# Eight forgetting-attention heads taken in pairs on TensorE, and one norm moved ahead of a weight split

## The reference

```
q, k, v, f_logit, cx, cb, cc, px, gate_logit = split(rmsnorm(x) @ w_in)
c = cumsum(log_sigmoid(f_logit + forget_b))            # 8 heads of 64
for the query blocks [0,128) (keys [0,128)) and [128,256) (keys [0,256)):
    p = softmax(q k^T / 8 + c_q - c_k, causal);  a = p @ v
y_attn = a @ w_attn_out
y_conv = (cb * conv3(cc * cx)) @ w_conv_out
y_pool = pooled_differences(px)[4 groups of 64] @ pool_w[group] * scale
g = sigmoid(gate_logit)                                # 3 x 1024
x = x + (g0*y_attn + g1*y_conv + g2*y_pool) @ w_o;  then a gated FFN
```

## Time and profile before

| | us |
|---|---|
| median of three runs | 1649.47 |
| the profiled execution, its own time | 1651.84 |
| its span, first to last instruction | 1650.0 |
| PE busy | 1585.8 |
| DVE busy | 1117.6 |
| ACT busy | 812.5 |
| POOL busy | 113.9 |

### The profile page before, as it was taken

How to read it: one execution, slowest core, us unless ns; L and a number is a source line. 1 busy time by engine, 2 the same in 40 slices (tenths; PEclk the granted TensorE clock), 3 DMA queues, 4 the chain that set the end, 5 groups by cost and what they waited for, 6 DMA issues and landing times.

```text
span 1650.0 us, 28888 instructions
## 1 busy us (share of the span) xinstructions
PE 1585.8 (96%) x12134; PEld 1485.1 (90%) x12134; DVE 1117.6 (68%) x1412; ACT 812.5 (49%) x1064; POOL 113.9 (7%) x107
## 2 busy tenths in 40 slices
PE   7999989999999999999988999999999999899998
PEld 6999989999899998999887989998999999789997
DVE  5767667775666767877577476666777756665554
ACT  5545444444545444444468454444455555454442
POOL 1040000000103000000011000000111102000000
PEclk9999999999999999999999899999999999899999
DMA  8765456667675636665632257675887655335652
GB/s 287 251 216 188 164 198 213 200 231 242 217 256 192 200 133 238 213 235 194 227 121 82 98 164 248 228 253 179 272 277 249 208 170 178 104 107 200 195 176 90
DMA packets 230497, 325.56 MB, mean 197 GB/s; under 512 B 7416, under 2 KB 195296, under 8 KB 230368
## 3 DMA queue, kind: packets, MB, share of 16 engines
q1 hardware_dynamic: 223304, 313.00, 56.3%
q10 hardware_dynamic: 7064, 10.71, 2.0%
HBM read 314.23 MB, written 9.45 MB: 196 GB/s over the span
## 4 chain that ended last, share of the span: by engine, by line
PE 77%; DVE 9%; ACT 5%; issue 4%; DMA 4%; POOL 1%; SPq 1%; DVEq 0%; ACTq 0%; POOLq 0%
PE bank L516 24%; PE bank L517 23%; PE bank L518 23%; DVE wlo L1576 2%; ACT whi L1117 2%; DMA raw<-in_w_in 1%; DMA raw<-in_w_ffn_in 1%; PE bank L559 1%; PE bank L593 1%; PE bank L925 1%; PE bank L909 1%; POOL rstd L1049 1%; PE bank L725 1%; PE bank L940 1%; DMA lbias<-forget_sums 1%
## 5 line engine op out<-in xcount | busy, mean ns | idle before, releaser
L1576 DVE TENSOR_TENSOR wlo<-raw,whi 128x2048 fp32r<-128x2048 f32 (+1 forms) x241 | 550.7, 2288 | 261.1 <-ACT whi L1117 260.9
L1117 ACT ACTIVATE whi<-raw 128x2048 fp32r<-128x2048 f32 (+1 forms) x241 | 456.0, 1895 | 119.1 <-PE bank L518 84.9
L516 PE MATMUL bank<-hT_hi,whi 128*128 128x256 f32 x1728 | 494.1, 286 | 6.9 <-DVE hT_lo L1691 3.0
L517 PE MATMUL bank<-hT_lo,whi 128*128 128x256 f32 x1728 | 488.8, 283 | 0.0
L518 PE MATMUL bank<-hT_hi,wlo 128*128 128x256 f32 x1728 | 488.8, 283 | 0.0
L516 PEld LDWEIGHTS bank<-hT_hi,whi 128*128 128x128 f32 x1728 | 331.1, 192 | 14.1 <-issue 10.1
L517 PEld LDWEIGHTS bank<-hT_lo,whi 128*128 128x128 f32 x1728 | 331.4, 192 | 1.2
L518 PEld LDWEIGHTS bank<-hT_hi,wlo 128*128 128x128 f32 x1728 | 331.3, 192 | 0.0
L516 PE MATMUL bank<-whi,hT_hi 128*128 128x256 f32 (+1 forms) x944 | 273.2, 289 | 5.3 <-DVE wlo L1576 2.5
L517 PE MATMUL bank<-wlo,hT_hi 128*128 128x256 f32 (+1 forms) x944 | 268.5, 284 | 0.0
L518 PE MATMUL bank<-whi,hT_lo 128*128 128x256 f32 (+1 forms) x944 | 268.3, 284 | 0.0
(11 more groups left out here) (280 smaller groups left out, 1525.5 us busy)
## 6 DMA issues: line engine op xcount, KB each, us to landing
raw<-in_mlp_w SPq DMA_DIRECT2D x64, 1024.0 KB, 5.7
ada_raw<-in_ada_w SPq DMA_DIRECT2D x96, 512.0 KB, 6.7
raw<-in_w_in SPq DMA_DIRECT2D x44, 1024.0 KB, 5.6
raw<-in_w_ffn_in SPq DMA_DIRECT2D x44, 1024.0 KB, 5.2
raw<-in_dil_w_in SPq DMA_DIRECT2D x36, 1024.0 KB, 5.5
raw<-in_w_ffn_out SPq DMA_DIRECT2D x22, 1024.0 KB, 4.8
raw<-in_w_o SPq DMA_DIRECT2D x8, 1024.0 KB, 5.2
biasb<-head_bias ACTq DMA_DIRECT2D x16, 512.0 KB, 4.6
```

The source lines that it names most:

```text
L516: pe.matmul(dst, lh, rh, start=start, stop=False)
L517: pe.matmul(dst, lh, rl, start=False, stop=False)
L1117: act.activation(view(whi[c % SPL], c), view(raw[c % RAW], c), ACT.Copy).then_inc(s_hi, 1)
L1576: dve.tensor_tensor(view(wlo[c % SPL], c), view(raw[c % RAW], c), view(whi[c % SPL], c).bitcast(F32), ALU.subtract).then_inc(s_lo, 1)
```

## The change

Heads and pooled groups are taken in pairs, the two of a pair in turn on two halves of the array: scores and pooled products on the two halves of its rows, values on the two halves of its columns. The values product swaps its operands, so its result comes out transposed, and `turn_pair` falls away; for this the probabilities are scaled by the inverted sums before they are transposed, with a semaphore `s_pn1` on which PE now waits. The four attention gates come last, with nothing between them. On ACT, `scores` splits the next chunk's weights before the exponentials. In `dilated`, `norm_probs` of the last pair stands ahead of `values(LAST, 0)` and `project_out(2, 3, 4, 5)`.

```diff
-            for i in range(H1 + 3):
-                if i < H1:
-                    begin_head(i)
-                if i <= H1:
-                    fill()
-                if 1 <= i <= H1:
-                    turn_probs(i - 1)
-                if i % 4 == 0:
-                    fill()
-                for gi in {3: (0,), 4: (1,), 5: (2, 3)}.get(i, ()):
-                    pool_branch(gi)
-                if 2 <= i < H1 + 2:
-                    values(i - 2)
-                if i in (4, 6, 8):
-                    turn_pair((i - 4) // 2)
-            last_gate(left.pop())
+            scores(0, left[0])
+            fill()
+            for p in range(H1 // 2):
+                norm_probs(p)
+                fill()
+                if p == 3:
+                    pool_branches(1)
+                turn_probs(p)
+                if p < H1 // 2 - 1:
+                    scores(p + 1, left[0])
+                if p == 2:
+                    pool_branches(0)
+                fill()
+                values(p)
+            while left:
+                fill()
...
             scores(LAST, 1, None)
             project_out(0, 1)
+            norm_probs(LAST, 1)
             values(LAST, 0)
             project_out(2, 3, 4, 5)
-            norm_probs(LAST, 1)
             turn_probs(LAST, 1)
```

On PE:

```diff
+                def scores(p, _):
+                    bks = [begin("a", ("S", unit1(l, 2 * p + h))) for h in range(2)]
+                    for q0, q1, c0 in ((0, P, 0), (P, S, P)):
+                        for h in range(2):
+                            rows = slice(64 * h, 64 * h + 64)
+                            m = pe.matmul(bks[h][:, c0:c0 + q1], qT1[rows, p, q0:q1], kT1[rows, p, 0:q1], start=True, stop=True)
...
+                def turn_probs(p):
+                    for h in range(2):
+                        u = unit1(l, 2 * p + h)
+                        pe.wait_ge(s_pn1, u + 1)
+                        bk = begin("a", ("T", u))
+                        for k in range(3):
+                            m = pe.transpose(bk[:, P * k:P * k + P], P1[h][:, P * k:P * k + P], ident[:, :])
...
+                def pool_branches(gp):
...
+                    bks = [begin("a", ("YP", l, 2 * gp + r)) for r in range(2)]
                     for half in range(2):
+                        for r in range(2):
+                            rows = slice(64 * r, 64 * r + 64)
+                            m = pe.matmul(bks[r][:, S * half:S * half + S], poolw[rows, gp, P * half:P * half + P],
+                                          pd[rows, gp, :], start=True, stop=True)
...
+                def values(p):
+                    for h in range(2):
+                        emptied(pe, ("T", unit1(l, 2 * p + h)))
+                    pair = unit1(l, 2 * p) // 2
+                    bk = begin("a", ("OT", pair))
+                    for t, kts in enumerate(((0,), (0, 1))):
+                        for kt in kts:
+                            for h in range(2):
+                                m = pe.matmul(bk[64 * h:64 * h + 64, P * t:P * t + P],
+                                              V1[:, kt, HD * (2 * p + h):HD * (2 * p + h) + HD],
+                                              PT1[h][:, P * (t + kt):P * (t + kt) + P], start=kt == 0, stop=kt == kts[-1])
```

On ACT and DVE:

```diff
+                def scores(p, following):
+                    split_ahead(("CO", l) if following is None else ("G", l, following))
+                    for h in range(2):
...
+                        exps(u, lambda t: L1[h][:, segs[t][0]:segs[t][1]], lambda t: P1[h][:, segs[t][0]:segs[t][1]])
...
+                def norm_probs(p):
+                    for h in range(2):
+                        u = unit1(l, 2 * p + h)
+                        dve.wait_ge(s_exp, 2 * u + 2)
+                        if u >= 2:
+                            dve.wait_ge(s_pn1, u - 1)
+                        dve.reciprocal(rz[:, h, :], zsum[:, h, :]).then_inc(s_rz, 1)
+                        dve.wait_ge(s_rz, u + 1)
+                        for t, (a, b) in enumerate(segs):
+                            ins = dve.tensor_scalar(P1[h][:, a:b], P1[h][:, a:b], rz[:, h, t:t + 1], None, ALU.mult)
+                        ins.then_inc(s_pn1, 1)
```

More of the change, by code:

```diff
@@ new lines, in values @@
+                def values(p):
[9 more added lines that the diff above has]
+                                              PT1[h][:, P * (t + kt):P * (t + kt) + P], start=kt == 0, stop=kt == kts[-1])
+                    end(m, ("OT", pair))
@@ L694, in _ @@
                 emptied(pe, ("qkT", 4 * l + 1))
-                forgetting_heads(begin_head, gate, conv_out, turn_probs, pool_branch, values,
-                                 lambda p: turn_pair(unit1(l, 2 * p) // 2),
-                                 lambda c: gate(c, lambda: turn_pair(unit1(l, 6) // 2)))
+                forgetting_heads(scores, gate, conv_out, idle, turn_probs, pool_branches, values)
                 for h in range(0, H1, 2):
@@ L1273, in _, with gate @@
                 act.activation(aT_hi[:, 4:6, :], cvb[:, :, :], ACT.Copy).then_inc(s_cvhi, 1)
-                def gate(c, between=idle):
+                def gate(c):
                     split_ahead(("G", l, c))
-                    between()
                     bk = full(act, ("G", l, c))
@@ L1295, in pool_branch @@
[L1295 to L1303, removed]
@@ L1308, in _ @@
+                forgetting_heads(scores, gate, lambda: split_ahead(("CO", l)), idle, turn_probs, pool_branches,
+                                 lambda p: at_high(unit1(l, 2 * p) // 2, p))
                 for c in range(2):
@@ L1824, in _, with scores @@
                 segs = ((0, P), (P, 3 * P))
[L1826 to L1839, removed]
+                def scores(p, _):
+                    for h in range(2):
+                        u = unit1(l, 2 * p + h)
+                        bk = full(dve, ("S", u))
+                        dve.wait_ge(s_lbias, u + 1)
+                        if p:
+                            dve.wait_ge(s_exp, 2 * (u - 2) + 2)
+                        for t, (a, b) in enumerate(segs):
+                            ins = dve.tensor_tensor_reduce(L1[h][:, a:b], bk[:, a:b], lbias[:, 2 * p + h, a:b], 1.0, NEG,
+                                                           ALU.add, ALU.max, mx[:, h, t:t + 1])
+                            if t == 0:
+                                link(ins)
+                        ins.then_inc(drain_sem(("S", u)), 1)
+                        emptied(dve, ("S", u))
+                        dve.tensor_scalar(nmax[:, h, :], mx[:, h, :], -1.0, None, ALU.mult).then_inc(s_nmax, 1)
@@ L1859, in conv_out, with pool_branches @@
                     split_ahead(("CO", l))
[L1861 to L1874, removed]
+                def pool_branches(gp):
+                    for gi in (2 * gp, 2 * gp + 1):
+                        emptied(dve, ("YP", l, gi))
+                        emptied(dve, ("G", l, 8 + gi))
+                        m2 = mg[:, 2 * gi:2 * gi + 2, :]
+                        dve.scalar_tensor_tensor(out=m2, in0=m2, scalar=1.0, in1=mt[gi % 2][:, :, :], op0=ALU.add,
+                                                 op1=ALU.mult).then_inc(s_ypused, 1)
+                forgetting_heads(scores, lambda c: split_ahead(("G", l, c)), conv_out, norm_probs, idle, pool_branches,
+                                 lambda p: at_low(unit1(l, 2 * p) // 2, p))
                 for c in range(1, 4):
```

90 lines of the change are left out of this document (37 added, 53 removed).

## The result

| | before | after |
|---|---|---|
| median of the timed runs, us | 1649.12 (1648.12 to 1651.09) | 1632.12 (1629.21 to 1633.72) |
| profiled execution, us | 1651.84 | 1629.21 |
| its span, us | 1650.0 | 1627.4 |

The ratio is 0.9894, 95% interval 0.9876 to 0.9911: 17.0 us faster, 2.7 more than the 14.3 forecast, and inside the range. The two profiled executions are 22.6 us apart. That is more than the medians, since the one of before is 2.7 above its median and the one of after 2.9 under its own.

A forecast was written before the change was run, and what follows sets the result against it. PE, busy 96% of the span, was taken as the bound. The terms 17.0 + 1.5 - 8.2 - 0.8 + 4.8 gave 14.3 us less, 1635.2 us for the median (chance 62%), range 1629 to 1642.

The forecast's parts named there:

- PE work, 17.0: Both forgetting layers: paired scores, values, pooled products and fewer tile changes save PE 8.5 us a layer, 17.0 in both.
- Old waits, 1.5: Second forgetting layer: PE's waits of 0.85 (low part of G10) and 0.69 us (weights' ring bank) both go.
- The new wait, 8.2: PE waits for DVE's scaling before pair 0's transposes: 3.2 us in the first layer, 5.0 in the second.
- none at pairs 2 and 3: Forgetting layers: PE does not wait for scaling there, as DVE finishes about 3 us before PE wants it.
- the 11 us: Upper size of the new wait over both layers, if each pair 0 scaling waits out a POOL sum.
- Clock in the second layer, 0.8: PE's clock may fall during the second forgetting layer's new wait: 0 to 3 us lost, 0.8 taken.
- The last pair, 4.8: Block 4's last dilated pair: PE's wait falls from 7.85 to 3.7 us; saving 4.2 to 6.2, 4.8 taken.
- the lower bound, 4.2: Block 4's last pair: low end of the 4.2 to 6.2 us saving, used where the clock stays low.
- (a): Small new wait of 5.4 us, clock held in both places: 19.3 us saved, 1630.2 us; chance 15%.
- (b): Long new wait of 11 us, low clock in second layer and block 4: 8.7 saved, 1640.8 us; chance 15%.
- (c): Array halves do not run together for these shapes: 14.3 us of saving gone, 1649.5 us; chance 4%.
- (d): The wait on `s_pn1` repeats at every pair, at 3.5 us a pair 28 lost: slower, 1655 us; chance 4%.

The follow-up runs named there:

- POOL held: Changed kernel with POOL held after each forgetting layer's first two biases until DVE has scaled the first pair: 1627.33 us, ratio 0.9857.
- the last pair alone: Kernel before with only the move of the last dilated pair's normalization: 1644.51 us, ratio 0.9976.
- the run with the low part first: Changed kernel, last dilated pair scaled ahead of chunks 0 and 1, DVE's low part and ACT's copies ahead of their splits: 1624.57 us, ratio 0.9846.
- the two parts timed alone: Changed kernel with the last dilated pair's normalization put back, 1633.44 us (15.5 faster); kernel before with only that move, 1644.51 us (4.5 faster).
- the run with the first pair scaled early: Changed kernel with DVE scaling each forgetting layer's first pair ahead of G10's low part and ada row: 1630.70 us.

## Why the prediction was right, and where it was off

- **PE work, 17.0 us.** Right. The stretches of the forgetting layers are 15.4 us shorter in the traces. The old waits of 1.5 are in this, and the small ones of 0.34 and 0.19 a layer, 1.1 in all, which the prediction left out. Against it stands the new wait, 3.3 as listed. The list misses a part of it: pair 0's transposes hold PE for 1.13 and 1.31 us up to the next group, where pairs 1 and 2 take 0.75, and so does pair 0 with POOL held. That is 0.4 and 0.6 more for head 1's scaling, of which 0.3 is listed. Counted so, the new wait is 3.9 and the work 15.4 - 1.5 - 1.1 + 3.9 = 16.7. The group times came out as worked out: scores of a pair 0.86 (0.85), values 0.81 (0.82), pooled pair 1.06. What the prediction did not see is that the values need their turns.
- **Old waits, 1.5.** Both gone. But they belong to late biases as much as to the code: in the other trace of the old order (the last pair alone) they stand in the first layer, 0.63 and 0.69, where the biases came 6.3 us behind PE's first scores, and not in the second, where it was 4.0. Where the biases come sooner, this term is worth nothing.
- **The new wait, 8.2.** This is the mis-sized term: 3.3 here, and 2.9 to 3.6 in the seven more traces of kernels that leave this wait as it is. The place, the cause and "none at pairs 2 and 3" were right. Of the 4.9 too many, 3.1 are in the second layer and 1.8 in the first.
  - Second layer, head 0: 3.7 forecast, 1.6 measured. The biases came 1.9 us behind PE's first scores (475.44 against 473.52), not 6.5, and DVE came to them from its convolution work: head 0's maximum stood 1.4 sooner than the earlier trace rows gave. The low part took 2.28, not 2.74, which is 0.5. PE came to the wait 0.15 later. The ada row (2.11) and the scaling of head 0 with its reciprocal (1.36 for 1.4) were sized rightly.
  - Head 1, both layers: 1.3 forecast each; 0.3 listed in the second and none in the first, 0.6 and 0.4 by the distances above. Its scaling took 0.73 and 0.55, and PE spends 0.55 on head 0's transposes meanwhile.
  - First layer, head 0: 1.9 forecast, 1.4 measured.

  The 6.5 was one execution. The old code has 4.0 in its other trace, and the twelve traces with the changed forgetting code have 1.3 to 2.6 in nine and 4.1 to 6.2 in three. Whether the change itself brings the biases forward, or only chance does, stays open.
- **POOL beside DVE.** The row (0.71 against 0.17) was read rightly as slowing, and holding POOL shows it: 0.55 against 1.35 for the same scaling. One scaling did wait for a pooled sum. In after's second layer, DVE's and POOL's timelines:

```profile
486.54 0.91 DVE L1852 TENSOR_SCALAR P<-P,rz 128x128 f32<-128x128 f32 x1
487.37 0.34 DVE L1852 TENSOR_SCALAR P<-P,rz 128x256 f32<-128x256 f32 x1
...
485.41 1.95 POOL L1082 TENSOR_TENSOR s<-s 128x540 f32<-128x540 f32 x1
```

The first instruction takes 0.91 where it takes 0.29 with POOL held, and the next begins at 487.37, when POOL's sum ends (485.41 + 1.95 = 487.36). DVE met the last 0.8 us of the sum, not the whole. No scaling of pair 0 in these traces was over 1.42 us, though POOL's sums are up to 3.0 long, so the 2.2 a head behind the 11 us did not come. The Trainium skill ("SBUF — State Buffer", "SBUF: two separate sides") has the two engines lock each other out for a whole instruction. At this place the trace agrees; what the forecast had too long is how much of POOL's instruction is left when DVE comes.
- **Clock in the second layer, 0.8.** Did not come: the granted clock is 1.00 from 484 to 492 us, through the wait of 1.6. The clock term was small either way.
- **The last pair, 4.8.** 3.8 in the traces and 4.5 timed. The wait fell to 3.7 as worked out; the clock fell in it, and the transposes stayed at 3.81. The earlier trace rows had said so: eight transposes in 1.94 after 3.71 idle are 0.24 each, the pace of sixteen in 3.81, where the full clock gives sixteen in 1.91 (the run with the low part first). The windows of the kernel before show the lower level there:

```profile
905.00:906.00 1.00, 0.00 (x0) 0.00 (x0) 0.97 (x5) 0.00 (x0) 0.00 (x0) 0.63 0.00 0
...
908.00:909.00 1.00, 1.00 (x6) 0.96 (x5) 0.64 (x3) 0.00 (x0) 0.00 (x0) 0.50 1.02 346
```

So the 0.6 us above the lower bound, 4.2, had no row for it. In the MLA stage PE was idle from 903.8 us and the clock fell at about 905.3; at the end of the dilated attention in after it was idle from 1409.4 and the clock fell at about 1412.1.

The sum with the sizes measured: 16.7 + 1.5 + 1.1 - 3.9 + 3.8 = 19.2, and 15.5 + 4.5 = 20.0 by the two parts timed alone. The median of the whole change is at 16.8 to 18.4 over the four comparisons, each with an interval of 2.5 to 3 us to either side. What separates them from the 19.2, 0.8 to 2.4 us, is within these intervals and stays open; one execution differs from another by more.

So the time came in its range with a forecast sum 4.9 us short of what the parts show. The wait was 4.3 too long by the distances (4.9 as listed), the small old waits of 1.1 were missing, and the clock in the second layer took 0.8 too much. The work (0.3 too much) and the last pair (1.0 too much) went the other way. That the measured 17.0 stands only 2.7 from the forecast of 14.3 is in part luck: the rest of the 4.9 is the part that stays open.

Rival (a), the small wait with the clock held in both places, gave 19.3 us, 1630.2. The measured 17.0 lies between it and the forecast, a little nearer to (a). Half of (a) came true, the wait (3.9, under its 5.4) but not the clock at block 4. (b), (c) and (d) did not come. Against (c), the pair's scores take one head's time; against (d), pair 1 waits only where PE does not wait at pair 0 and DVE is late beside POOL, as in the run with the first pair scaled early.

## What to carry to other kernels

- When a change adds a wait for an engine with a queue of its own, size it from more than one execution: the arrival that starts that queue (here a DMA, 1.3 to 6.5 us behind PE in the same stage over fourteen traces) moved by more than the instructions in it did.
- Moving the awaited step ahead in a full queue only hands the wait to the next one (1.4 and 1.9 at pair 0 became 1.2 and 1.0 at pair 1 in one run, 1.6 and 2.2 in another). Taking away what slows the queue, here POOL at its side, took it away, but for 0.8 and 0.5 in an execution with late biases.
- A wait of a few us can cost nearly as much again in clock. Here 3.7 us of idle time cost 6.8, and the last of it was in two other queues' order, found only after the first wait was gone.

## What had not been expected of the hardware

- Two heads' matmuls on the two row halves run together even when issued one head after the other (0.86 either way). On the column halves they lose a third (1.08 against 0.81).
- After 3.7 us of idle time PE was granted half the clock at the end of the dilated attention, and went on at half until 1418.9 us, 5.8 us into work. After 2.34 us in the same place it kept 1.00. The kernel before shows the same in the MLA stage: 3.71 us idle, then 0.50.
- POOL pays for DVE as DVE for POOL: the first layer's eight biases take 5.60 us in the kernel before and 8.69 in after, where DVE's low part, ada row and scaling run beside them (6.72 in the second layer).
